# RWKV scan: the unused semaphore increment ahead of each TensorE job is taken out, and waits on one counter are merged

## The reference, cut to what matters

```python
def step(S, inp):
    r_t, w_t, k_t, v_t, kk_t, b_t = inp
    sa = jnp.einsum('bhij,bhj->bhi', S, -kk_t)
    S = (S * w_t[:, :, None, :] + sa[..., None] * b_t[:, :, None, :]
         + v_t[..., None] * k_t[:, :, None, :])
    y = jnp.einsum('bhij,bhj->bhi', S, r_t)
    return S, y
_, y = lax.scan(step, S0, xs)
```

## Time and profile before

| | us |
|---|---|
| median of three runs | 2990.99 |
| lowest and highest run | 2988.66, 2993.97 |
| the profiled execution, its own time | 2987.43 |
| its span in the trace | 2985.6 |

### The profile page before, as it was taken

One profiled execution on the slowest core, in us unless ns is written; L12 is line 12 of the kernel. 1 busy time (PEld: TensorE's weight loads), 2 busy tenths in 40 slices (PEclk: granted clock), 3 DMA queues, 4 the chain that ended last, 5 costly groups with the idle time before them and its releaser, 6 DMA issues.

```text
span 2985.6 us, 47079 instructions
## 1 busy us (share of the span) xinstructions
PE 2879.9 (96%) x19488; PEld 2335.2 (78%) x19488; DVE 976.1 (33%) x1447; ACT 947.3 (32%) x1102; POOL 1362.8 (46%) x1111
## 2 busy tenths in 40 slices
PE   8999999999999998898999999999999999999998
PEld 6768778888788886677887788887888877788887
DVE  3441342223312126435553412116211146331213
ACT  3243232123312236632332322224222236422222
POOL 5454444444444444233332444445444457544444
PEclk9999999999999999998999999999999999999999
DMA  5202222222222221441111122222222220122222
GB/s 190 95 21 93 98 86 99 97 91 94 99 99 85 102 109 59 181 153 42 46 46 69 72 97 99 99 99 85 99 99 99 86 101 30 71 85 99 92 91 85
DMA packets 43424, 271.65 MB, mean 91 GB/s; under 512 B 4832, under 2 KB 4960, under 8 KB 13824
## 3 DMA queue, kind: packets, MB, share of 16 engines
q1 hardware_dynamic: 40032, 252.64, 23.5%
q10 hardware_dynamic: 3232, 16.65, 1.4%
HBM read 254.59 MB, written 14.68 MB: 90 GB/s over the span
## 4 chain that ended last, share of the span: by engine, by line
issue 45%; POOL 30%; PE 21%; DVE 2%; POOLq 0%; DVEq 0%; DMA 0%; ACT 0%; SPq 0%; ACTq 0%
POOL w_lo L558 29%; PE ps L890 6%; PE ps L701 3%; PE ps L702 3%; PE ps L703 3%; PE ps L843 1%; POOL ybuf L633 1%; PE ps L875 1%; PE ps L862 1%; PE ps L798 1%; PE ps L770 1%; POOL x_res L669 0%; PE ps L914 0%; DVE work L1741 0%; DVEq L1738 0%
## 5 line engine op out<-in xcount | busy, mean ns | idle before, releaser
L558 POOL TENSOR_TENSOR w_lo<-w_raw,w_hi 128x512 fp32r<-128x512 f32 x876 | 1119.1, 1310 | 1348.1 <-ACT w_hi L1209 1348.1
L701 PE MATMUL ps<-act_hi,w_hi 128*128 128x512 f32 x2240 | 881.4, 393 | 31.0 <-DVE act_lo L1682 16.0
L702 PE MATMUL ps<-act_lo,w_hi 128*128 128x512 f32 x2240 | 875.4, 391 | 0.0
L703 PE MATMUL ps<-act_hi,w_lo 128*128 128x512 f32 x2240 | 875.1, 391 | 0.0
L1209 ACT CAST w_hi<-w_raw 128x2048 fp32r<-128x2048 f32 x219 | 417.9, 1908 | 1014.1 <-PE ps L703 986.8
L701 PEld LDWEIGHTS ps<-act_hi,w_hi 128*128 128x128 f32 x2240 | 422.6, 189 | 133.8 <-issue 34.8
L703 PEld LDWEIGHTS ps<-act_hi,w_lo 128*128 128x128 f32 x2240 | 422.7, 189 | 89.1
L702 PEld LDWEIGHTS ps<-act_lo,w_hi 128*128 128x128 f32 x2240 | 423.0, 189 | 88.1 <-issue 1.2
L701 PE MATMUL ps<-hid_hi,w_hi 128*128 128x512 f32 x1184 | 463.6, 392 | 9.2 <-POOL w_lo L558 8.5
L703 PE MATMUL ps<-hid_hi,w_lo 128*128 128x512 f32 x1184 | 461.5, 390 | 0.0
L702 PE MATMUL ps<-hid_lo,w_hi 128*128 128x512 f32 x1120 | 436.4, 390 | 0.0
(11 more groups left out here) (266 smaller groups left out, 2354.2 us busy)
## 6 DMA issues: line engine op xcount, KB each, us to landing
w_raw<-stream SPq DMA_DIRECT2D x223, 1024.0 KB, 4.8
spill<-work ACTq DMA_DIRECT2D x3, 2048.0 KB, 9.0
scratch<-spill SPq DMA_DIRECT2D x24, 256.0 KB, 4.7
work<-bias_in SPq DMA_DIRECT2D x1, 3072.0 KB, 17.5
work<-spill SPq DMA_DIRECT2D x12, 256.0 KB, 3.4
x_res<-x_in SPq DMA_DIRECT2D x4, 512.0 KB, 7.4
spill<-work ACTq DMA_DIRECT2D x2, 1024.0 KB, 5.1
spill<-area ACTq DMA_DIRECT2D x1, 2048.0 KB, 10.2
```

The costliest lines, as they stand in the source:

```text
L558: inst = tt(w_lo[:, s, a:a + 512], w_raw[:, s, a:a + 512], w_hi[:, s, a:a + 512].bitcast(F32), ALU.subtract)
L701: mm(out, wh, hi[:, k, :], start=(k == 0) if begin is None else begin, stop=False)
L702: mm(out, wh, lo[:, k, :], start=False, stop=False)
L703: return mm(out, wl, hi[:, k, :], start=False, stop=end)
```

## The change

Three edits. The semaphore pe_waited and the function waited() go, with its call at the end of ready(). The waits that come from NEEDS and BANKS_BEFORE are first collected in a dictionary that keeps the highest value for each counter; then made() is called once for each counter. made() itself, the order of the jobs and all other waits stay.

```diff
-            "job_mm", "dve_jobs", "act_jobs", "pe_waited",
+            "job_mm", "dve_jobs", "act_jobs",
...
-            def waited():
-
-                pe.sem_inc(S["pe_waited"], 1)
-
...
                     if kind == "bonus":
                         pe.wait_ge(S["rkw_made"], m + 1)
+                    counts = {}
                     for need in NEEDS.get(kind, ()):
-                        made(*OUT[need, m])
+                        engine, count = OUT[need, m]
+                        counts[engine] = max(count, counts.get(engine, 0))
                     for last, tile in BANKS_BEFORE.get((kind, m), ()):
                         for part in results_of(last):
-                            made(*OUT[part, tile])
-                    waited()
+                            engine, count = OUT[part, tile]
+                            counts[engine] = max(count, counts.get(engine, 0))
+                    for engine, count in counts.items():
+                        made(engine, count)
```

## The result

| | before | after |
|---|---|---|
| median of 5 runs, us | 2990.84 | 2975.04 |
| lowest and highest, us | 2988.66, 2993.97 | 2970.72, 2977.47 |
| the profiled execution, us | 2987.43 | 2977.47 |
| its span, us | 2985.6 | 2975.7 |

The ratio is 0.9946, with a 95% interval of 0.9932 to 0.9961: 16.2 us faster (11.7 to 20.3). The two profiled executions are 10.0 us apart, since the one of before was among its faster runs and the one of after was its slowest; the sizes that follow from the traces are therefore on the low side.

The account below looks back on a forecast made before the run. TensorE was taken as the bound, held in the scan by waits, instruction packets and a DMA loop. The middle of 3.3 and 9.2 us, 6.2, less a third, rounded to 4.0 us saved: 2987.0 us, range 2980 to 2994 us.

Parts of the forecast that it names:

- The three holds: In the scan, TensorE is held by waits for VectorE, late instruction packets, and a loop through other engines and a DMA.
- The other places earn nothing: Scan jobs where the event instruction runs ahead of its job, hidden by TensorE's backlog: priced at 0.
- 63 places: Scan places where the first load follows the last event by 0.08 us: together worth 3.3 to 9.2 us.
- The prices at real waits: Where TensorE stands at a real wait in the scan: 0.06 us saved per single job, 0.21 per pair, by closer reading.
- The third loop: Group norm of tile m-2, then decay tile's DMA, then VectorE's scan: absorbs savings over 11 us of each 31 to 36.
- the third that was taken off: Share of the scan's saving held to be covered by the wait for the decay tile: 6.2 us became 4.1 us.
- The instruction supply: TensorE running out of instructions in the scan: absorbs some saving, and one packet less gives back up to 3.6 us.
- The clock: Granted clock in the scan, 0.92 of full speed: credited 0, with a fall more or fewer worth 3 us.
- (a): Scan saving vanishes in stands behind instruction packets and the decay tile's DMA: under 1.5 us, 2990.3 us; chance 0.20.
- (d): Builder still puts an event ahead of every job with a wait: 1 to 2 us saved, 2989.5 us; chance 0.05.
- (c): Slower: waits in scan weight loads stop later loads being brought forward, net loss 5.0 us, 2996 us; chance 0.09.
- (b): All scan savings outside the third loop arrive, 6.1 us, plus one clock fall fewer, 3 us: about 2982 us; chance 0.20.

Follow-up runs that it names:

- Experiment 9: Changed kernel with three increments ahead of each of the 79 jobs that wait for nothing; 2990.21 us, ratio 0.9997.
- 12: Changed kernel with six increments between the chunks of each C, Yo, X, XT, Kv and KKT job, 288 in all; 2997.72 us, ratio 1.0016.
- 8: Changed kernel with 748 increments among the 512-column matmuls of the streamed slabs, none in the scan; 2975.12 us, ratio 0.9939.
- experiment 3: Changed kernel with its 304 increments put back, but behind the last matmul of each job; 2985.77 us, ratio 0.9986.
- 4: Kernel before with two increments ahead of each job instead of one; 3003.63 us, ratio 1.0045.
- Experiment 13: Changed kernel with three increments ahead of each of 72 jobs in the part held to be covered, 216 in all; 2983.39 us, ratio 0.9976.
- the padded one: Changed kernel and kernel before, each with 128 increments at TensorE's very start; 2985.69 us (0.9976) and 2999.45 us (1.0030).
- Experiment 7: Changed kernel with the second job's waits of each pair right ahead of its own first matmul; 2974.40 us, ratio 0.9946.
- experiment 14: Changed kernel with each pair's second waits later and three thrown-away matmuls on constants ahead of LX1; 2966.94 us, ratio 0.9912.

## Why the prediction was wrong

**What bounds the scan.** The three holds that it named are in the trace. What it missed is a fourth, which mostly leaves no hole right behind it: the issue of the sequencer's own instructions, those of L881.

**The step that failed** is "The other places earn nothing: there the event runs ahead of its job". It priced 63 places out of some 220 and left the others at zero. Experiment 9 shows 0.064 us each at jobs that wait for nothing, 12 shows 0.073 us each in the midst of jobs. At 1435.3 the event does run 0.2 us ahead of its job. I read the picture of one place as if a lead were a cover. The account that fits, argued and not shown, is that a spent lead is missed later, when a packet of instructions comes late; the same instruction costs nothing in the slabs (8). With 246 instructions gone, 16.2 us are 0.066 us each, within what 3, 4, 9, 12 and 13 give (0.040 to 0.073).

**The prices at real waits** were right: 0.04 us forecast after L1997, 0.05 measured, and 0.27 before. As a part of the whole, the wait's place is worth 4.2 us (1.2 to 6.9) by experiment 3, against 4.4 + 1.0 in the part of the sum for fresh waits.

**The covers.** The third loop acts as a cover, and the third that was taken off is near its share: 97 of the scan's 276 us gained nothing in either pair, and VectorE stood 4.5 us longer for the DMA. TensorE did not stand longer, as the prediction had it: its idle time in these rounds went from 9.1 to 7.4 us. Experiment 13 put increments into the covered part of every round and cost 9.0 us; but in the rounds where the DMA is late it cost nothing that can be seen. So the cover is seen in whole rounds of the middle of the scan and not in a third of each round. Nor is their length fixed: doubled increments lengthened them to 107.1 us, fillers shortened them to 91.0, which is why TensorE's own work must be a part of the loop. It was taken off a sum that was too small; this is not what failed.

**The instruction supply** is the second step that failed. The prediction had it absorb part of the saving, and sized what it gives back by the number of packets, one fewer, up to 3.6 us. The number did go from 60 to 59, but the idle time behind packets fell by 12.0 us in this pair and by 6.2 us in the padded one, with 60 and 59 packets too. It is where most of the lost idle time had been. How the issue of an event and the wait for a packet add up was not separated by a run; it is the point that stays open. A page that hides all fetching behind the dispatch (the Trainium skill, Runtime: NRT & Kernel Launch, "Instruction fetch mechanics") disagrees with these holes still: 18.7 us of them before, 6.7 after.

**The count.** 53 event instructions were forecast to stay, 69 did: the waits of a pair meet ahead of one load. Experiment 7 brings them to 54 and gains nothing that can be seen.

**The clock** was left out of the sum, with a fall more or fewer in the range. The profiled scans had 0.91 and 0.89; experiment 14 gained 10.2 us on the changed kernel with a higher clock, more than the whole change as forecast.

**The rivals.** (a) is out as the whole account, though its DMA is real in three rounds; (d) is out, since L881 is gone. (c), waits in loads being dearer, is out: experiment 3 has them cheaper. (b) is the nearest: that everything outside the third loop arrives is what the traces show, but its 6.1 us for it were too few, and the fall of the clock that it spared did not come, the clock went from 0.91 to 0.89.

## What to carry to other kernels

Where many small matmuls follow each other, count the sequencer's own instructions (waits, increments) and price each, at 0.03 to 0.07 us here as an average over the scan; a lead seen at one place is not a cover. A cover is a stretch whose length does not change; look for it between two marks in both traces. Test that with a dose: the same instruction doubled, moved behind, and put into a stage of long matmuls tells number, place and stage apart. When an engine stands regularly behind another, see what the granted clock does after it before calling the stand harmless.

## What the runs showed of the hardware that was not expected

- Two event instructions in a row start 0.15 us apart, though each shows 0.051 us; the load behind the last starts 0.08 us after its start. A load that carries its own wait starts 0.04 to 0.05 us after the releaser.
- 748 event instructions among 512-column matmuls cost nothing that can be seen (0.9939 against 0.9946); 288 among the scan's small ones cost 20.9 us.
- TensorE's idle time 1.2 to 1.8 us behind the end of an instruction packet was 18.7 us of the scan before and 6.7 us after, with 60 and 59 packets; with 288 event instructions in the midst of jobs it was 22.7 us.
- 128 of them at the start of the program delayed the first matmul by 12 us; the 128 started within 19.4 us, one each 0.15 us.
- With three thrown-away matmuls of 256 columns ahead of each of seven jobs, the granted clock of the scan was 0.97, where it was 0.89 without, and the time 10.2 us shorter.
